# The mixer's output projection as seven block products, and all early down-weight differences in the second projection

## The reference

```python
h = x + jnp.concatenate([out_a, out_b, out_c], axis=-1) @ lw['w_o']
h = h + memory_attend(rmsnorm(h, lw['norm_mem_g']), mem_k, mem_v, lw)   # q = hn @ w_mq, ..., o @ lw['w_mo']
u, ffn_buf_new = causal_dwconv(rmsnorm(h, lw['norm_ffn_g']) @ lw['w_up'], ffn_buf, lw['w_ffn_conv'])
ug, uv = split_cols(u, (D_FF, D_FF))
h = h + (jax.nn.silu(ug) * uv) @ lw['w_down']
```

## Time and profile before

| | us |
|---|---|
| median of 3 runs | 1820.46 (1814.69 to 1822.42) |
| the profiled execution's own time | 1819.15 |
| its span | 1817.8 |
| "wo" stage, first matmul to last | 629.7 to 731.1 |
| "mo" stage, first matmul to last | 950.0 to 1052.6 |

### The profile page before, as it was taken

One profiled execution on the slowest core, in us unless ns is written; L12 is line 12 of the kernel. 1 busy time (PEld: TensorE's weight loads), 2 busy tenths in 40 slices (PEclk: granted clock), 3 DMA queues, 4 the chain that ended last, 5 costly groups with the idle time before them and its releaser, 6 DMA issues. The chain is left out here.

```text
span 1817.8 us, 27740 instructions
## 1 busy us (share of the span) xinstructions
PE 1751.4 (96%) x10342; PEld 1602.9 (88%) x10342; DVE 1141.0 (63%) x1354; ACT 782.3 (43%) x1489; POOL 767.2 (42%) x644
## 2 busy tenths in 40 slices
PE   6999999999989999999999989999999999999998
PEld 5999999988867788898788879999999999988887
DVE  6325765765666632413536288888888888677874
ACT  5126773325566432312143255444444444443441
POOL 4001212014444272212127428766666666448642
PEclk9999999998989999999999999999999999999999
DMA  6222111224245263124516722222222222397753
GB/s 169 80 56 62 42 36 49 84 85 122 60 135 191 94 234 121 47 105 145 192 68 210 254 67 73 72 72 72 72 72 72 72 72 72 136 377 236 243 190 121
DMA packets 173569, 215.06 MB, mean 118 GB/s; under 512 B 14695, under 2 KB 122600, under 8 KB 171648
## 3 DMA queue, kind: packets, MB, share of 16 engines
q1 hardware_dynamic: 172560, 213.55, 36.0%
q0 software_dynamic: 896, 0.19, 0.1%
q10 hardware_dynamic: 16, 0.00, 0.0%
HBM read 167.11 MB, written 46.60 MB: 118 GB/s over the span
## 5 line engine op out<-in xcount | busy, mean ns | idle before, releaser
L3901 PE MATMUL ffn_banks<-h_parts,up_hi 128*128 128x384 f32 x1920 | 488.7, 335 | 7.6 <-DVE h_parts L4397 4.5
L3901 PEld LDWEIGHTS ffn_banks<-h_parts,up_hi 128*128 128x128 f32 x1920 | 345.7, 188 | 9.7 <-issue 7.8
L3901 PE MATMUL ffn_banks<-h_parts,up_lo 128*128 128x384 f32 x960 | 320.7, 334 | 0.0
L4287 POOL TENSOR_TENSOR up_lo<-up_raw,up_hi 128x512 fp32r<-128x512 f32 x172 | 258.5, 1518 | 105.2 <-ACT up_hi L4056 74.5
L1000 PE MATMUL proj_banks<-x_hi,in_w_hi 128*128 128x384 f32 x624 | 212.6, 341 | 0.5 <-DVE x_lo L251 0.5
L1000 PE MATMUL proj_banks<-x_hi,in_w_lo 128*128 128x384 f32 x624 | 208.7, 334 | 0.0
L1000 PE MATMUL proj_banks<-x_lo,in_w_hi 128*128 128x384 f32 x624 | 208.6, 334 | 0.0
L3901 PEld LDWEIGHTS ffn_banks<-h_parts,up_lo 128*128 128x128 f32 x960 | 180.2, 188 | 0.0
L4337 POOL TENSOR_TENSOR h_parts<-down_cells,h_parts 128x512 fp32r<-128x512 f32 x69 | 103.2, 1499 | 90.4 <-ACT h_parts L4125 90.3
L4012 PE MATMUL ffn_banks<-h_parts,up_hi 128*128 128x512 f32 x352 | 137.1, 390 | 0.0
L4015 PE MATMUL ffn_banks<-h_parts,up_lo 128*128 128x512 f32 x352 | 137.0, 389 | 0.0
(11 more groups left out here) (574 smaller groups left out, 3803.4 us busy)
## 6 DMA issues: line engine op xcount, KB each, us to landing
up_raw<-in_w_up SPq DMA_DIRECT2D x44, 512.0 KB, 3.9
up_raw<-ffn_gated_rows SPq DMA_DIRECT2D x44, 320.0 KB, 5.8
ffn_gated_rows<-h SPq DMA_DIRECT2D x22, 576.0 KB, 2.8
in_w_raw<-in_w_in SPq DMA_DIRECT2D x24, 512.0 KB, 4.0
down_cells<-down_sums SPq DMA_DIRECT2D x44, 256.0 KB, 4.1
up_raw<-ffn_gated_rows SPq DMA_DIRECT2D x33, 256.0 KB, 3.5
down_sums_cells<-in_w_down SPq DMA_DIRECT2D x7, 1024.0 KB, 6.5
down_sums<-down_sums_cells SPq DMA_DIRECT2D x7, 1024.0 KB
```

Source lines behind the costliest of these rows:

```text
L3901: ins = nc.tensor.matmul(banks[:, bank, 0:TC], wt[:, j, k, :], parts[:, q, x, k, :], start=(fresh and n == 1), stop=(n == last), skip_grou ...
L4287: nc.gpsimd.tensor_tensor(w_lo[:, j], weights.full(j), w_hi[:, j].bitcast(F32), ALU.subtract).then_inc(weights.split[j], 1)
```

## The change

The "wo" stage gets a function of its own, `block_projection`. Of the nine row tiles, tiles 0 to 3 ("near") and 4 to 7 ("far") form the two row halves of a 2 x 2 block matrix, whose column halves are the weights' slices 0 to 3 and 4 to 7; the weights are cut in two by slices and in two by columns. In place of eight products of blocks there are seven, whose operands are sums and differences of blocks; each of the seven (`P_Q1` to `P_Q4`, in the order Q1, Q5, Q6, Q3, Q2, Q7, Q4) runs over four row tiles, four slices and three parts. The ninth tile (the sample rows, "odd") is computed without sums, in four pieces, inside Q1, Q5, Q3 and Q2. VectorE forms the sums of the activations in the place of the memory's values and keys, GpSimd the differences of the weights in place; ScalarE makes all high parts. Q5's bank is added to two places of `h`, all others to one. Q1, Q6, Q7 and Q4 run on a chain in banks 0 to 3, which keep their sum from one to the next; Q5, Q3 and Q2 take turns in banks 4, 5 and 7. High and low parts have two places per operand, so those of a product are made once the one before the last is done.

The weight slices 3 to 7 are loaded at once, into room of their own and into the place of the query weights, whose load comes later. All 11 steps of `DownSums` are formed in the "mo" stage, through three slots: 0 and 1 by VectorE, 2 and 3 after GpSimd's low parts of the seventh tile, 4 after those of the eighth, 5 to 10 after those of the ninth.

The core of the new function (the setup of names and memory is left out):

```diff
+        def takes_of(n, j):
+
+            if j == TILES:
+                return {P_Q1: ((odd, L),), P_Q5: (), P_Q3: ((odd, R),), P_Q2: ((odd, L),)}[n]
+            return {P_Q1: ((near + j, L),), P_Q5: ((near + j, R), (far + j, R)), P_Q6: ((near + j, R),), P_Q3: ((near + j, R),),
+                    P_Q2: ((near + j, L),), P_Q7: ((far + j, R),), P_Q4: ((far + j, L),)}[n]
...
+        @block.sync
+        def _(sp):
+            for k in range(3, KD):
+                sp.dma_start(w[k], load_rest(k)).then_inc(w_landed[k - 3], 16)
+            for t in (*range(near, near + TILES), odd, *range(far, far + TILES)):
+                sp.dma_start(out[:, t, :], residual[t]).then_inc(r_landed[t], 16)
+            sp.wait_ge(stored_too, 32)
+            sp.wait_ge(b_split, HK * P_Q4)
+            for n in range(then.weights.RING):
+                then.weights.load(sp, n)
...
+            def bank_free(n, j):
+
+                if j == TILES:
+                    if n != P_Q1:
+                        pe.wait_ge(taken, TAKEN[P_Q3 if n == P_Q2 else P_Q1, TILES])
+                elif n in ON_X:
+                    if n != P_Q1:
+                        pe.wait_ge(taken, TAKEN[ON_X[ON_X.index(n) - 1], j])
+                else:
+                    c = Y_TILES.index((n, j))
+                    if c >= 3:
+                        pe.wait_ge(taken, TAKEN[Y_TILES[c - 3]])
...
+            for n in BLOCK_PASSES:
+                for j in range(TILES + 1):
+                    if (n, j) not in DONE or (n == P_Q1 and j < TILES):
+                        continue
+                    bank_free(n, j)
+                    if j == TILES:
+                        pe.wait_ge(odd_split, 1 if n in (P_Q1, P_Q5) else 2)
+                    for k in range(HK):
+                        if j == 0:
+                            pe.wait_ge(a_split, HK * n + k + 1)
+                            pe.wait_ge(b_split, HK * (n - 1) + k + 1)
+                        turn = 2 * (j - 2) + k // 2 if n == P_Q7 else 4 + 2 * j + k // 2
+                        if n in (P_Q7, P_Q4) and k % 2 == 0 and 0 <= turn < KD:
+                            turn_early(turn)
+                        for i in range(3):
+                            ins = one(n, j, k, i)
+                    ins.then_inc(done, 1)
...
+            def wait_slot(n):
+                if n >= 2:
+                    act.wait_ge(done, PASS_DONE[n - 2])
...
+            for n in BLOCK_PASSES[1:6]:
+                wait_slot(n)
+                for k in range(HK):
+                    high_b(n, k)
+                    high_a(n, k)
+                if n == P_Q5:
+                    high_odd(1)
+            for t in range(3):
+                sum_of_squares(t)
+            act.wait_ge(summed, 3)
+            then.lengths(0)
+            wait_slot(P_Q4)
+            for k in range(HK):
+                high_b(P_Q4, k)
+                high_a(P_Q4, k)
+            sum_of_squares(3)
...
+            for k in range(HK):
+                form(k, P_Q5)
+            for k in range(HK):
+                low_b(P_Q5, k)
+            for k in range(HK):
+                form(k, P_Q6)
+            for k in range(HK):
+                low_b(P_Q6, k)
+            for k in range(HK):
+                form(k, P_Q7)
+            for n in (P_Q3, P_Q2):
+                for k in range(HK):
+                    low_b(n, k)
...
+            for k in range(HK):
+                low_a(P_Q1, k)
+                dve.wait_ge(b_high, k + 1)
+                nc.vector.tensor_tensor(b_lo[:, at(P_Q1, k), :], b_cell(P_Q1, k), b_hi[:, at(P_Q1, k), :].bitcast(F32),
+                                        ALU.subtract).then_inc(b_split_first, 1)
+            low_odd(0)
+            dve.wait_ge(stored_too, 32)
+            for k in range(HK):
+                form(k, P_Q5)
+            for k in range(HK):
+                low_a(P_Q5, k)
+            for k in range(HK):
+                form(k, P_Q6)
+            low_odd(1)
+            for k in range(HK):
+                form(k, P_Q7)
+            for j in range(TILES + 1):
+                take(P_Q1, j)
+            for n in (P_Q5, P_Q6, P_Q3, P_Q2):
+                for j in range(TILES):
+                    low_a(n + 1, j)
+                    if n == P_Q5:
+                        form(j, P_Q3)
+                    take(n, j)
+                take(n, TILES)
+            for k in range(HK):
+                low_a(P_Q4, k)
+            dve.wait_ge(b_split, HK * (P_Q7 - 1) + HK)
+            dve.wait_ge(t_formed, 4 * HK)
+            then.scale(dve, 0)
+            for j in range(TILES):
+                take(P_Q7, j)
+                for i in ((), (0, 1), (2, 3), (4,))[j]:
+                    then.early_low(dve, i, done)
+            for j in range(TILES):
+                for i in ((5,), (6, 7), (), ())[j]:
+                    then.early_low(dve, i, done)
+                take(P_Q4, j)
+                if j == 2:
+                    then.scale(dve, 1)
...
-                for k in steps[t:t + 1] if 2 <= t < len(steps) else ():
-                    next_sums(k)
+                for k in {1: (2,), 2: (3,), 3: (4,), 4: (5, 6), 5: (7, 8), 6: (9, 10)}.get(t, ()):
+                    beside.store_and_load(sp, k)
...
-                for k in by_pool[0:2] if t == 6 else by_pool[2:3] if t == 7 else by_pool[3:] if t == 8 else ():
+                for k in {6: (2, 3), 7: (4,), 8: range(5, beside.STEPS)}.get(t, ()):
```

More of the change, by code:

```diff
@@ L442, in first_weights, with wait_low_free @@
         pass
-    def wait_low_free(self, dve, k, projected):
-        if k == 0:
+    def wait_low_free(self, dve, k, done):
+        if k == self.ORDER[0]:
             dve.wait_ge(self.C.keys_stored, 16)
[L447 to L456, removed]
+        if k < 2:
+            dve.wait_ge(done, self.LOW_FREE_AT)
     def turn(self, pe, i):
@@ L2760, in row_projection @@
             then.early_banks = banks
-        by_vector, by_pool = ((), steps) if residual else (steps[0:2], steps[2:])
         summed = ph.sem(f"{tag}_summed")
@@ L2781, in _ @@
         def _(sp):
[L2782 to L2786, removed]
             if not loaded:
                 weights.load_first(sp)
-            if not residual:
-                for k in steps[0:2]:
-                    beside.load(sp, k)
+            for k in range(2):
+                beside.load(sp, k)
             weights.load_rest(sp, w_split)
@@ L2795, in _ @@
                 sp.dma_start(out[:, t, :], rows).then_inc(r_landed[t], 16)
-                if t == together - 1:
-                    sp.wait_ge(stored_too, 32)
-                    sp.wait_ge(stored, 16)
-                    for k in steps[0:2]:
-                        beside.load(sp, k)
-            for k in steps if residual else steps[0:2]:
-                next_sums(k)
+            sp.wait_ge(w_split, KD + 1)
+            beside.load(sp, 2)
+            for k in range(2):
+                beside.store_and_load(sp, k)
             if then and not kept:
@@ L2927, in _ @@
                 low_slice(k)
-            for k in by_vector:
+            for k in range(2):
                 beside.form(dve, nc.vector, k)
@@ L4723, in program @@
         query_rows = QueryRows(nc, C, query_phase, "mq_norm", h, V_MEM, hn_hi, hn_lo, [w_o.raw[:]], w_mq)
-        row_projection(nc, C, "wo", C.mixT, NT, w_o, h, C.h_sums, residual=x_tiles, loaded=True,
-                       squares=M["mem"][:, :, 256:768], stored=C.keys_stored, stored_too=C.memory_stored,
-                       then=query_rows, beside=C.down_sums, steps=WO_SUMS)
+        mem_cells = M["mem_out"].rearrange("p (s k c) -> p s k c", s=2, k=KD // 2)
+        block_projection(nc, C, "wo", C.mixT, 0, 4, 8, (w_o.raw, w_mq.raw[:].rearrange("p r k c -> p r (k c)")), w_o.wait,
+                         (mem_cells[:, 0], mem_cells[:, 1]), h, C.h_sums, x_tiles, M["mem"][:, :, 256:768], C.keys_stored,
+                         C.memory_stored, query_rows, lambda k: w_o.slices[k])
         mix.close()
@@ L4763, in program @@
         row_projection(nc, C, "mo", attnT, NT, w_mo, h, C.h_sums, loaded=True, kept=(C.h_kept, C.h_stored), then=feed_rows,
-                       order=(6, 7, 8, 0, 1, 2, 3, 4, 5), beside=C.down_sums, steps=MO_SUMS)
+                       order=(6, 7, 8, 0, 1, 2, 3, 4, 5), beside=C.down_sums)
         attn.close()
```

232 lines of the change are left out of this document (216 added, 16 removed).

## The result

The changed kernel takes **1859.35 us** (median of 6 runs, 1856.42 to 1861.04) against 1818.32 for the kernel before in the same series: ratio **1.0224**, 95% interval 1.0207 to 1.024, so 41 us slower. The forecast was 1833 with a range of 1815 to 1841: the sign was right, the size was not. The profiled execution has a span of 1859.8.

The account below looks back on a forecast made before the run. The prediction took PE to bound the output projection outright. Its terms, -10.9 + 16.0 + 4.3 + 1.5 + 3.2 + 0.5 = +14.6 us on 1819.15, gave 1833.8; it forecast 1833, own range 1826 to 1839, 8-in-10 range 1815 to 1841.

Parts of the forecast that it names:

- Taken away, 10.9 us: Output projection: 384 matmuls in place of 432, 48 x 0.2267 = -10.9 us; the eight transpose groups stay.
- The first gap, 16.0 us: Output projection, second product's fourth tile: PE waits for VectorE's late bank additions, loss 16.0 us.
- The turn: Output projection: a VectorE and a GpSimd subtraction meeting take 1.55 us, ends 1.45 and 1.87.
- The rival of full turns: VectorE's and GpSimd's operations overlap nothing, 6.7 us more, 1840 us; chance 0.09.
- The scalings, 4.3: Before the early transposes: row scalings stand behind four low parts of the last product on VectorE, loss 4.3 us.
- The stage's end, 1.5: Output projection's end: ACT squares the last tile late, ahead of the query projection's first conversion, loss 1.5 us.
- The clock, 3.2: Output projection: granted clock falls behind each of two long gaps, 1.6 us each, loss 3.2, ends 0 and 6.4.
- the first half: The forecast's terms ahead of the second projection, from matmuls taken away to the clock: 14.1 us in sum.
- The second projection, 0.5: Second projection: row scalings meet POOL, loss 0.5 us, between 0 and 3; the 11 weight differences hide.
- The loads keep pace: Second projection: a slot's round of forming, storing and loading is 15.7 us over three slots, 5.2 a difference.
- that hides, with 3 us to spare: Second projection's end: last store lands at about 1047, ACT's conversions follow while PE works until 1052.6.
- up to 4: Second projection's end: cost of overrunning the 3 us, if the last store takes twice its 4.1 us and more.

Follow-up runs that it names:

- POOL short: Changed kernel with most of GpSimd's subtractions in the output projection cut from 512 columns to 8, leaving the result incomplete: 1837.7 us, ratio 1.01.
- experiment 2: Changed kernel with the second projection of the kernel before, first four differences left out, so the block products alone: 1835.4 us, ratio 1.0078.
- experiments 7: Changed kernel with the three row scalings ahead of the last product's four low parts on VectorE: 1855.4 us, ratio 1.0187.
- 10: Changed kernel without ScalarE's sum of squares of the eighth row tile; single run: PE's wait at the query projection 1.8 us in place of 3.0.
- Experiments 1: Kernel before with only the change's second projection, all 11 weight differences formed there over three slots: 1844.3 us, ratio 1.0127.
- experiment 3: Changed kernel, SyncE waiting for the store before the newest, so two stores may be under way: 1845.3 us, ratio 1.0145.
- 9: Kernel before with all 11 differences in the second projection, stores a step ahead, third and fourth difference formed early: 1825.5 us, ratio 1.0033.

## Why the forecast was wrong

*Taken away, 10.9 us.* Right: 384 matmuls. With POOL short, PE was busy for 92.2 us in the stage, against 0.2267 x 384 + 8 x 0.37 = 90.0.

*The first gap, 16.0 us.* Right in place and cause, a little short in size. PE went on 39.9 us after its first matmul, forecast 37.8; less 96 x 0.2267 that is a loss of 18.1. The waits show only 14.2 + 1.4 of it. The rest is PE at the lower clock (0.56 from 634 to 636: the stage's first 12 matmuls took 4.40 us for 2.72), which the forecast didn't have and which costs nothing, since VectorE's queue sets when PE goes on: in experiment 2 the same 12 matmuls took 3.3 us, and PE went on after 39.9 us as well. The turn was under-sized, 1.71 for 1.55; 16 operations met a full one, where 17 were forecast. The median of the feed-forward stage, from which 1.55 was taken, stands between a least of 0.68 and 1.25 and a most of 1.78 and 2.47, so it mixes met and unmet operations and was no price of a meeting. The rival of full turns had 1.87: the truth lies halfway.

*The scalings, 4.3:* 4.6. *The stage's end, 1.5:* 1.2 more at the query projection's start. Both right; experiments 7 and 10 show their causes.

*The clock, 3.2.* The 12 matmuls behind the first gap took 5.07 us (673.84 to 678.91) where 2.72 is their time at full clock, so 2.4 for one gap, forecast 1.6. Behind the scalings six took 2.71 us (730.42 to 733.13) for 1.36, another 1.4: 3.8 for the two gaps, within the range given. One more fall, in the query projection, wasn't forecast and costs 1.5. In sum the first half was forecast at 14.1 and measured 18.2.

*The second projection, 0.5.* **This is the step that failed**: "The loads keep pace", with a slot's round of 15.7 us "over three slots, 5.2 a difference", and from it "that hides, with 3 us to spare". Three slots divide a round only if three rounds are under way. SyncE's program has one: it waits for the store it just issued before it loads, and issues the next store behind that load. The period was 10.1 us, nearly that of before with two slots, so the third slot brought nothing. With four more differences the last came 46 us after the forecast's 1047 (some 22 of these are the shift of the whole stage), and PE waited 21.5 us. No rival named this; the cap of "up to 4" rested on the same period. Experiments 1 to 3 and 9 show it: alone it costs 19.6 us in its stage, stores a step ahead give 14 back, an earlier begin another 1.8 to 2.5.

The 4.3 us ahead of the output projection stay open: a difference of two single executions within a spread of 9.

## What to carry to other kernels

A ring of slots has the pace of its most serial queue. Read the period of a repeated step from the trace where it already waits for transfers, and not as the sum of its parts divided by the slots. And before matmuls are traded for additions, add up what VectorE and GpSimd would do at the price they have beside each other: here 50 and 40 small operations, many of them at 1.7 us, cost 28 us in a stage from which 48 matmuls had taken 11, and 19 of the 28 went when GpSimd's were shortened.

## What the runs showed of the hardware

VectorE's and GpSimd's additions and subtractions of 128x512, all operands in SBUF, took 1.70 to 1.72 us each when both engines had a row of them, where alone they took 0.60 and 1.27: the sum is 1.87, the longer one 1.27. VectorE's bank additions, with one operand in PSUM, kept their 0.60 beside the same GpSimd operations (five in 3.07 us from 668.20, with GpSimd at work until 670.6). The Trainium skill (SBUF — State Buffer, section "SBUF: two separate sides") has the lock last the whole instruction; the trace stays 0.16 us per pair short of that.

A 1 MB store issued right behind a 1 MB load landed after 8.6 us (median of the changed kernel), the loads after 6.2 to 6.4; where it was issued ahead of the load (experiment 3), after 5.3 to 5.5, and the loads took 7.9 to 9.4. With two stores under way the mean rate over 65 us was 319 GB/s in place of 261 (1019 to 1084 in the changed kernel).
